# The first weight group behind three norms, multiplied one token tile at a time

## The chip, the cores and the metric

The kernel runs on one core of one Trainium2 chip. The metric is the device time of one execution in microseconds, as the median of several runs. A profile of one execution stands beside it.

## The reference

Two transformer-like blocks run one after the other on 256 tokens of width 1024, all in float32. What matters here is the place where a residual stream is normed and then multiplied by weights. In short:

```
# block 1
hx = modulate(rmsnorm(x, pre_mix_g), sh1, sc1);  yx = mlstm_mixer(hx, hc, ...)
x  = x + g1 * rmsnorm(yx, post_mix_g)            # "post1"
hx = modulate(rmsnorm(x, pre_ffn_g), sh2, sc2)   # "norm2"
yx = (silu(conv3(hx @ up_gate)) * (hx @ up_u)) @ down_w
x  = x + g2 * rmsnorm(yx, post_ffn_g)            # "post2"
# block 2
h  = rmsnorm(x, attn_norm_w)                     # "norm3"
x  = x + (delta-rule heads and forgetting attention of h @ w_in) @ w_out
h  = rmsnorm(x, ffn_norm_w)                      # "norm4"
x  = x + (silu(h @ gate) * (h @ up)) @ w_down
x  = x + sigmoid(rmsnorm(x, ple_norm_w) @ w_ple_gate) * (p @ w_ple_proj)   # "norm5"
out = rmsnorm(x, final_norm_w)
```

## The kernel before

The 256 tokens are two token tiles of 128 (`TT = 2`); the width is eight slices `k` of 128 (`KD = 8`). Every product with a weight is made of three float32r products: the weight and the activation are each split in a high part (`w_hi`, `h_hi`) and a low remainder (`w_lo`, `h_lo`), and high times high, high times low and low times high are summed in PSUM. Weights come in groups of 1 MB through a ring of three buffers. For each group SyncE issues the DMA, ScalarE casts it to `w_hi` (L623 or L631), VectorE subtracts to get `w_lo` (L1141 or L1149), and TensorE multiplies. Each engine has one program written out by hand, and semaphores order them; an engine never goes past a wait.

A norm in front of a product goes like this. ScalarE takes sums of squares (L641), GpSimd makes the reciprocal root (L447 and L450), and VectorE scales the identity by it into `diag` (L1171), once per token tile. TensorE multiplies `x` by `diag`, which transposes and scales at once (`transposed`, L1845). ScalarE writes `h_hi` from PSUM with gain and shift (`hi_T`, L672 or L674), and VectorE writes `h_lo` (`transposed`, L1161 and L1162 for norm2, L1164 for norms 3 and 4). In all of this a step covers one slice `k` with both token tiles, 256 columns, and a PSUM bank holds two slices of both tiles. So `h_hi` can't begin before the transposes of token tile 1.

The first group behind a norm is multiplied in `feature_tiles` with `ready` set: 32 products with `h_hi` (L1819 and L1820), then 16 with `h_lo` (L1826), each with a 128x128 piece of weights standing in the array and 256 token columns moving. Norms 2 and 4 are followed by a loop over pairs of groups (`ffn`, `rounds`: three rounds of three pairs as a hardware loop, then two pairs written out), norm 3 by the groups of the `gdn` stage.

In front of norms 2 and 3 stands another norm (`post_norm`): VectorE multiplies the product in PSUM by a gain (L1178), and adds it, scaled, to `x` (L1188). It does so for tile 0 and then tile 1, since the last two weight groups in front of it are multiplied tile by tile. Norm 4 has only a residual sum in front of it (L1677).

Of the kernel before, what the change touches and what calls it, by code (L numbers as in the profile page):

```python
# [131 lines left out]
def two_blocks(nc, I, out):  # L132
# [5 lines left out]
    with ExitStack() as ctx:  # L138
# [20 lines left out]
        for kind, n in (("tr", KD // 2), ("hi", KD), ("hT", KD)):  # L159
            FAMILY[kind] = (("norm1", KD), ("y1", n), ("norm2", n), ("norm3", n), ("mix", KD // 2), ("norm4", n),  # L160
                            ("norm5", n))
# [192 lines left out]

        def in_round(s, r):


            return (s + 2 * ROUND * r, 0) if isinstance(r, int) else (s, r)

        def rounds(eng, step):  # L360

            with eng.Fori(0, ROUNDS) as r:
# [250 lines left out]
        def _(act):  # L613
# [35 lines left out]
            def post_norm(post, norm, product, bank0, updates):  # L649
# [26 lines left out]


# [149 lines left out]
            post_norm("post1", "norm2", "mix_out", 2, 0)  # L827
            hi_T("norm2", NORM_BANKS["norm2"], scale=lambda k: mod2[:, KD + k:KD + k + 1], shift=lambda k: mod2[:, k:k + 1])
# [22 lines left out]
            post_norm("post2", "norm3", "down", 4, 4)  # L851
# [9 lines left out]
            hi_T("norm3", NORM_BANKS["norm3"], lambda k: pcol("attn_norm", k))  # L861
# [187 lines left out]
            for i in range(4):  # L1049
                norm_half("norm4", 8, i, i // 2, i % 2)  # L1050
# [3 lines left out]
            hi_T("norm4", NORM_BANKS["norm4"], lambda k: pcol("ffn_norm", k))  # L1054
# [56 lines left out]
        def _(dve):  # L1111
# [61 lines left out]
            def post_norm(post, norm, gain, bank0):  # L1173
# [252 lines left out]
            post_norm("post1", "norm2", gp1, 2)  # L1426
            dve.sem_inc(S("act_full"), ROUND)
            transposed("norm2", NORM_BANKS["norm2"], lambda k: mod2[:, KD + k:KD + k + 1], lambda k: mod2[:, k:k + 1])
# [35 lines left out]
            post_norm("post2", "norm3", gp2, 4)  # L1464


            transposed("norm3", NORM_BANKS["norm3"], lambda k: pcol("attn_norm", k))
# [213 lines left out]
            transposed("norm4", NORM_BANKS["norm4"], lambda k: pcol("ffn_norm", k))  # L1681
# [46 lines left out]
        def _(pe):  # L1728
# [77 lines left out]
            def feature_tiles(s, bank, r=0, ready=None, between=None):  # L1806
# [5 lines left out]
                if ready is not None:  # L1812
                    for f in range(2):
                        fs_ = slice(f * P, (f + 1) * P)
                        for k in range(KD):
                            if f == 0:
                                pe.wait_ge(S("hi"), base("hi", ready) + k + 1)
                            dst = ps[:, bank, f * T:(f + 1) * T]
                            pe.matmul(dst, hi[:, k, fs_], h_hi[:, k, :], start=f == k == 0, stop=False)  # L1819
                            pe.matmul(dst, lo[:, k, fs_], h_hi[:, k, :], start=False, stop=False)  # L1820
                    for f in range(2):
                        fs_ = slice(f * P, (f + 1) * P)
                        for k in range(KD):
                            if f == 0:
                                pe.wait_ge(S("hT"), base("hT", ready) + k + 1)
                            ins = pe.matmul(ps[:, bank, f * T:(f + 1) * T], hi[:, k, fs_], h_lo[:, k, :], start=False,  # L1826
                                            stop=f == 1 and k == KD - 1)
                    ins.then_inc(group_used, 1)
                    return
                for f in range(2):  # L1830
# [296 lines left out]
            def ffn(name, norm):  # L2127

                def step(r, u):
                    pe.wait_ge(S("act_full"), base("act_full", name) + ROUND * r + u + 1)  # L2130
                    for half in range(2):
                        feature_tiles(at[name][2 * u + half], 2 * u + half, r, norm if u == half == 0 else None)

                rounds(pe, step)
# [16 lines left out]
            transposed("norm2")  # L2151
# [4 lines left out]
            transposed("norm3")  # L2156
            def gdn_tiles(j, between=None):
# [3 lines left out]
                feature_tiles(at["gdn"][j], j % 2, ready="norm3" if j == 0 else None, between=between)  # L2161
# [44 lines left out]
            gdn_tiles(0)  # L2206
# [192 lines left out]
            def att_out(i, t):  # L2399
# [5 lines left out]
                for kk in range(GH):  # L2405
                    if n == 0 and t == 0 and kk % 2 == 0:
# [41 lines left out]
            for t in range(TT):  # L2448
                att_out(2, t)
                att_out(3, t)  # L2450
# [49 lines left out]
```

## Time and profile before

| | us |
|---|---|
| median of 3 runs | 849.33 (847.73 to 855.03) |
| the profiled execution's own time | 849.84 |
| span of its profile, first to last instruction | 848.1 |
| TensorE matmul busy | 803.2 (95%) |
| VectorE busy | 509.9 (60%) |
| ScalarE busy | 386.2 (46%) |
| mean granted TensorE clock | 0.988 |

TensorE is busy nearly all the time, so what counts is where it stands idle, how long each matmul takes from one start to the next, and how many there are. Busy time of TensorE counts overlapping matmuls once, and their ends are modelled, so the start times in the timeline say more than the busy share.

### The profile page before, as it was taken

Reading aid. Unit: us, or ns where it says so; the run is one execution under the profiler, and the core shown is the slowest. Engines: PE = TensorE matmul, PEld = TensorE weight load, DVE = VectorE, ACT = ScalarE, POOL = GpSimd, SP = SyncE. Lnnn points to the kernel's source line nnn. Section 1 sums busy time; section 2 is a strip of 40 time slices with the busy share of each in tenths; the row PEclk is TensorE's granted clock in tenths of the full one; section 3 lists DMA queues with packets and bytes.
Section 4 is the critical chain, followed back from the end, with each engine's and each line's share of the span. In section 5 each row is a group of like instructions: output and inputs, shape, how many; then the busy total and the mean of one; then the engine's idle time right before and its main releaser. Section 6 shows DMA issues by size and latency. Waiting matters only on the chain. (4 is left out here: it accounts for less than half of the span.)

```text
span 848.1 us, 12688 instructions
## 1 busy us (share of the span) xinstructions
PE 803.2 (95%) x5135; PEld 711.2 (84%) x5135; DVE 509.9 (60%) x681; ACT 386.2 (46%) x522; POOL 105.6 (12%) x170
## 2 busy tenths in 40 slices
PE   3899999999899999999979999999999999999996
PEld 1678877777789999987779988988899999988885
DVE  0447789866676766686467884454464554554355
ACT  1533413344554565434366544546364344343373
POOL 3210221501100000000070314110100000000000
PEclk9999999999999999999999999999999999999999
DMA  9767377723165555577624343311455555455531
GB/s 329 271 205 278 123 256 258 278 71 96 54 199 188 166 169 186 185 274 271 189 80 133 100 149 100 100 51 50 149 187 176 172 197 189 162 170 196 175 100 49
DMA packets 102430, 142.74 MB, mean 168 GB/s; under 512 B 6248, under 2 KB 62065, under 8 KB 102385
## 3 DMA queue, kind: packets, MB, share of 16 engines
q1 hardware_dynamic: 96128, 136.33, 48.0%
q10 hardware_dynamic: 6192, 5.79, 2.2%
q8 instruction: 31, 0.51, 0.3%
q14 instruction: 15, 0.11, 0.0%
q0 software_dynamic: 64, 0.01, 0.0%
HBM read 141.05 MB, written 1.05 MB: 168 GB/s over the span
## 5 line engine op out<-in xcount | busy, mean ns | idle before, releaser
L1732 PE MATMUL ps<-h_hi,w_hi 128*128 128x256 f32 x720 | 205.2, 285 | 0.9 <-DVE w_lo L1141 0.9
L1733 PE MATMUL ps<-h_lo,w_hi 128*128 128x256 f32 x720 | 204.4, 284 | 0.0
L1734 PE MATMUL ps<-h_hi,w_lo 128*128 128x256 f32 x720 | 204.4, 284 | 0.0
L1141 DVE TENSOR_TENSOR w_lo<-raw,w_hi 128x2048 fp32r<-128x2048 f32 (+1 forms) x63 | 139.8, 2226 | 75.0 <-ACT w_hi L623 74.7
L623 ACT CAST w_hi<-raw 128x2048 fp32r<-128x2048 f32 (+1 forms) x63 | 116.8, 1854 | 101.4 <-PE ps L1734 56.5
L1732 PEld LDWEIGHTS ps<-h_hi,w_hi 128*128 128x128 f32 x720 | 138.9, 193 | 1.1 <-DVE w_lo L1141 1.1
L1733 PEld LDWEIGHTS ps<-h_lo,w_hi 128*128 128x128 f32 x720 | 138.9, 193 | 0.0
L1734 PEld LDWEIGHTS ps<-h_hi,w_lo 128*128 128x128 f32 x720 | 138.8, 193 | 0.0
L1149 DVE TENSOR_TENSOR w_lo<-raw,w_hi 128x2048 fp32r<-128x2048 f32 x44 | 100.7, 2290 | 61.4 <-ACT w_hi L631 61.4
L631 ACT CAST w_hi<-raw 128x2048 fp32r<-128x2048 f32 x44 | 83.6, 1899 | 52.6 <-PE ps L1734 52.6
L1732 PE MATMUL ps<-w_hi,h_hi 128*128 128x512 f32 x208 | 84.9, 408 | 2.8 <-DVE r L1342 1.6
L1733 PE MATMUL ps<-w_lo,h_hi 128*128 128x512 f32 x208 | 82.3, 396 | 0.0
L1734 PE MATMUL ps<-w_hi,h_lo 128*128 128x512 f32 x208 | 82.1, 395 | 0.0
L1732 PE MATMUL ps<-w_hi,act_hi 128*128 128x512 f32 x176 | 70.1, 398 | 0.0
L1733 PE MATMUL ps<-w_lo,act_hi 128*128 128x512 f32 x176 | 69.6, 395 | 0.0
L1734 PE MATMUL ps<-w_hi,act_lo 128*128 128x512 f32 x176 | 69.6, 395 | 0.0
L1732 PEld LDWEIGHTS ps<-w_hi,h_hi 128*128 128x128 f32 x208 | 39.7, 191 | 15.6 <-issue 3.4
L1734 PEld LDWEIGHTS ps<-w_hi,h_lo 128*128 128x128 f32 x208 | 39.7, 191 | 8.8
L1733 PEld LDWEIGHTS ps<-w_lo,h_hi 128*128 128x128 f32 x208 | 39.7, 191 | 7.6
L447 POOL TENSOR_SCALAR ss<-ss 128x1 f32<-128x1 f32 x14 | 4.4, 315 | 301.1 <-ACT junk L641 300.9
L1732 PEld LDWEIGHTS ps<-w_hi,act_hi 128*128 128x128 f32 x176 | 33.1, 188 | 8.2 <-issue 0.2
L1733 PEld LDWEIGHTS ps<-w_lo,act_hi 128*128 128x128 f32 x176 | 33.1, 188 | 8.0 <-issue 0.2
(365 smaller groups left out, 1265.2 us busy)
## 6 DMA issues: line engine op xcount, KB each, us to landing
raw<-in_ada_w SPq DMA_DIRECT2D x24, 1024.0 KB, 5.5
raw<-in_ffn_up_w SPq DMA_DIRECT2D x22, 1024.0 KB, 5.1
raw<-in_w_gate_up SPq DMA_DIRECT2D x22, 1024.0 KB, 5.1
raw<-in_w_in SPq DMA_DIRECT2D x14, 1024.0 KB, 5.2
raw<-in_m_in_w SPq DMA_DIRECT2D x12, 1024.0 KB, 5.2
raw<-in_ffn_down_w SPq DMA_DIRECT2D x10, 1024.0 KB, 5.2
raw<-in_w_down SPq DMA_DIRECT2D x10, 1024.0 KB, 5.0
raw<-in_m_out_w SPq DMA_DIRECT2D x4, 1024.0 KB, 5.4
```

Of the source, the lines that this page charges most:

```text
L447: link(pool.tensor_scalar(s, s, ss[:, c0 + TT:c0 + TT + 1], EPS, ALU.add, ALU.add))
L623: act.copy(part_view(w_hi, s), raw_view(split[s])).then_inc(hi_ready, 1)
L631: act.copy(part_view(w_hi, s), raw_view(split[s])).then_inc(hi_ready, 1)
L1141: dve.tensor_tensor(part_view(w_lo, s), raw_view(split[s]), part_view(w_hi, s).bitcast(F32), ALU.subtract).then_inc(lo_ready, 1)
L1149: dve.tensor_tensor(part_view(w_lo, s), raw_view(split[s]), part_view(w_hi, s).bitcast(F32), ALU.subtract).then_inc(lo_ready, 1)
L1732: pe.matmul(dst, l_hi, r_hi, start=first, stop=False)
L1733: pe.matmul(dst, l_hi, r_lo, start=False, stop=False)
L1734: return pe.matmul(dst, l_lo, r_hi, start=False, stop=last)
```

## The change

Behind norms 2, 3 and 4 the work goes by token tile. The transposes of tile 0 go to two PSUM banks and those of tile 1 to two others (`tile_bank`). `h_hi` and `h_lo` are written for 128 columns at a time (`tile_hi`, `tile_lo`), with twice as many instructions, and the first weight group is multiplied first with tile 0 and then with tile 1: 2 x 48 matmuls of 128 columns where there were 48 of 256 (`first_group`). ScalarE writes tile 0's `h_hi` between the sums of squares of tile 1's product and of tile 1's `x`. VectorE writes six of the eight `h_lo` slices of tile 0 after tile 1's `x` update, then makes tile 1's `diag`, then the last two. In norm 4 the transposes of tile 0 stand in the middle of the last part of the attention's output product (`att_out(3, 1, between)`), and VectorE makes `diag` and `h_lo` of tile 0 ahead of tile 1's residual sum. In TensorE's program the first round of the two `ffn` loops is written out, since only it has the first group; the rounds that follow use the plain order of products.

```
+        def tile_bank(name, t, k):
+            return ps[:, NORM_BANKS[name][2 * t + k // 4], k % 4 * P:(k % 4 + 1) * P]
...
-        def rounds(eng, step):
+        def rounds(eng, step, unrolled=0):
+            for r in range(unrolled):
+                for u in range(ROUND):
+                    step(r, u)
+            with eng.Fori(unrolled, ROUNDS) as r:
...
# ScalarE, post_norm
                         sum_sq(ps[:, bank0 + 2 * n + t, :], SS[post] + TT * n + t)
+                        if n == t == 1:
+                            tile0_hi()
                         if n == 1:
                             for half in range(2):
                                 norm_half(norm, updates, 2 * t + half, t, half)
...
+            def tile_hi(name, t, scale, shift=None):
+                tok = slice(t * P, (t + 1) * P)
+                for k in range(KD):
+                    act.wait_ge(S("tr"), base("tr", name) + 2 * t + k // 4 + 1)
+                    src = tile_bank(name, t, k)
+                    if shift is None:
+                        ins = act.activation(h_hi[:, k, tok], src, ACT.Copy, scale=scale(k))
+                    else:
+                        ins = act.activation(h_hi[:, k, tok], src, ACT.Identity, scale=scale(k), bias=shift(k))
+                    ins.then_inc(S("hi"), 1)
...
# ScalarE, norm 4
-            for i in range(4):
-                norm_half("norm4", 8, i, i // 2, i % 2)
+            for i in range(2):
+                norm_half("norm4", 8, i, 0, i)
+            tile_hi("norm4", 0, lambda k: pcol("ffn_norm", k))
+            for i in range(2, 4):
+                norm_half("norm4", 8, i, 1, i - 2)
...
# VectorE
+            def tile_lo(name, t, scale, shift=None, ks=range(KD)):
+                tok = slice(t * P, (t + 1) * P)
+                for k in ks:
+                    dve.wait_ge(S("hi"), base("hi", name) + t * KD + k // 4 * 4 + 4)
+                    src = tile_bank(name, t, k)
+                    hi = h_hi[:, k, tok].bitcast(F32)
+                    if shift:
+                        link(dve.tensor_scalar(full[:, k, tok], src, scale(k), shift(k), ALU.mult, ALU.add))
+                        ins = dve.tensor_tensor(h_lo[:, k, tok], full[:, k, tok], hi, ALU.subtract)
+                    else:
+                        ins = dve.scalar_tensor_tensor(h_lo[:, k, tok], src, scale(k), hi, ALU.mult, ALU.subtract)
+                    ins.then_inc(S("hT"), 1)
...
# VectorE, post_norm, behind the x updates of tile t
+                    if t == 1:
+                        tile0_lo(range(0, 6))
                     diagonal(norm, t, base("rstd", post) + 2 * t + 2)
+                tile0_lo(range(6, KD))
...
# VectorE, norm 4, in the loop of residual sums over t
-            for t in range(TT):
-                diagonal("norm4", t, base("rstd", "norm4") + t + 1)
+                if t == 0:
+                    diagonal("norm4", 0, base("rstd", "norm4") + 1)
+                    tile_lo("norm4", 0, lambda k: pcol("ffn_norm", k))
+            diagonal("norm4", 1, base("rstd", "norm4") + 2)
...
# TensorE
+            def tile_turned(name, t):
+                pe.wait_ge(S("diag"), base("diag", name) + t + 1)
+                for k in range(KD):
+                    ins = pe.matmul(tile_bank(name, t, k), x[:, t, k * P:(k + 1) * P], diag[:, t, :], start=True, stop=True)
+                    if k % 4 == 3:
+                        ins.then_inc(S("tr"), 1)
+
+            def tile_products(name, t, s, bank):
+                hi, lo = weights(s)
+                tok = slice(t * P, (t + 1) * P)
+                for k in range(KD):
+                    pe.wait_ge(S("hi"), base("hi", name) + t * KD + k + 1)
+                    for f in range(2):
+                        dst, fs_ = ps[:, bank, f * T + t * P:f * T + (t + 1) * P], slice(f * P, (f + 1) * P)
+                        pe.matmul(dst, hi[:, k, fs_], h_hi[:, k, tok], start=t == f == k == 0, stop=False)
+                        pe.matmul(dst, lo[:, k, fs_], h_hi[:, k, tok], start=False, stop=False)
+                for k in range(KD):
+                    pe.wait_ge(S("hT"), base("hT", name) + t * KD + k + 1)
+                    for f in range(2):
+                        dst, fs_ = ps[:, bank, f * T + t * P:f * T + (t + 1) * P], slice(f * P, (f + 1) * P)
+                        ins = pe.matmul(dst, hi[:, k, fs_], h_lo[:, k, tok], start=False, stop=t == f == 1 and k == KD - 1)
+                return ins
+
+            def first_group(name, s, bank, turned=0):
+                for t in range(TT):
+                    if t >= turned:
+                        tile_turned(name, t)
+                    ins = tile_products(name, t, s, bank)
+                ins.then_inc(group_used, 1)
...
# TensorE, att_out(3, 1): the last product ahead of norm 4
-                att_out(3, t)
-            transposed("norm4")
-            ffn("gate_up", "norm4")
+                att_out(3, t, (lambda: tile_turned("norm4", 0)) if t else None)
+            ffn("gate_up", "norm4", 1)
```

## Rows read from the trace of the kernel before

**Rows 1.** The page, part 1: busy time, share of the span, instructions.

```profile
PE 803.2 (95%) x5135; PEld 711.2 (84%) x5135; DVE 509.9 (60%) x681; ACT 386.2 (46%) x522; POOL 105.6 (12%) x170
```

**Rows 2.** Waits: who waited for whom, us in total, times, longest.

```profile
PE ps L1845 <- DVE diag L1171: 10.0, 5, 3.3
PEld ps L1732 <- issue: 3.7, 6, 1.5
```

**Rows 3.** Timeline of TensorE at norm 2: start, us, line, out<-in, count, idle before.

```profile
220.32 2.05 PE L1845 MATMUL ps<-diag,x 128*128 128x128 f32 x16 [0.35 <-DVE diag L1171]
225.64 2.76 PE L1845 MATMUL ps<-diag,x 128*128 128x128 f32 x16 [3.27 <-DVE diag L1171]
228.05 0.56 PE L1819 MATMUL ps<-h_hi,w_hi 128*128 128x256 f32 x1
...
237.12 0.58 PE L1732 MATMUL ps<-h_hi,w_hi 128*128 128x256 f32 x1 [0.87 <-DVE w_lo L1141]
```

**Rows 4.** Timeline of ScalarE and VectorE at norm 2.

```profile
222.75 0.63 ACT L641 ACTIVATE junk<-x 128x512 f32<-128x512 f32 x1 [1.99 <-DVE x L1188]
226.39 3.76 ACT L674 ACTIVATE h_hi<-ps,mod 128x256 fp32r<-128x256 f32 x8 [0.23 <-PE ps L1845]
...
221.90 1.41 DVE L1188 SCALAR_TENSOR_TENSOR x<-full,rstd,x 128x512 f32<-128x512 f32 x2 [0.42 <-POOL rstd L450]
227.44 0.54 DVE L1161 TENSOR_SCALAR full<-ps,mod 128x256 f32<-128x256 f32 x1 [1.86 <-ACT h_hi L674]
...
234.78 4.49 DVE L1141 TENSOR_TENSOR w_lo<-raw,w_hi 128x2048 fp32r<-128x2048 f32 x2
```

**Rows 5.** Windows: us, busy by engine, granted clock, DMA share, GB/s.

```profile
228.00:230.20 2.20, 2.20 (x12) 2.20 (x12) 2.11 (x6) 2.20 (x6) 0.00 (x0) 0.50 0.00 0
```

**Rows 6.** Groups of instructions by shape: busy us, mean ns of one, idle before.

```profile
L1733 PE MATMUL ps<-h_lo,w_hi 128*128 128x256 f32 x720 | 204.4, 284 | 0.0
L1733 PE MATMUL ps<-w_lo,h_hi 128*128 128x512 f32 x208 | 82.3, 396 | 0.0
L1732 PEld LDWEIGHTS ps<-h_hi,w_hi 128*128 128x128 f32 x720 | 138.9, 193 | 1.1 <-DVE w_lo L1141 1.1
L1929 PEld LDWEIGHTS ps<-h_lo,wg_parts 128*32 128x32 f32 x16 | 1.7, 108 | 0.1
L641 ACT ACTIVATE junk<-ps 128x512 f32<-128x512 f32 x8 | 4.8, 598 | 10.0 <-PE ps L1734 9.9
L641 ACT ACTIVATE junk<-ps 128x128 f32<-128x128 f32 x8 | 2.2, 276 | 2.1 <-PE ps L2441 1.9
L1585 DVE SCALAR_TENSOR_TENSOR r<-ps,neg_c 128x256 f32<-128x256 f32 x8 | 3.3, 415 | 0.0
L1585 DVE SCALAR_TENSOR_TENSOR r<-ps,neg_c 128x128 f32<-128x128 f32 x8 | 2.3, 291 | 17.8 <-PE ps L2290 17.8
```

**Rows 7.** Timeline of TensorE's weight loads early in the kernel.

```profile
32.63 0.97 PEld L1885 LDWEIGHTS ps<-row_of,r 128*128 128x128 f32 x8 [0.19 <-DVE r L1204]
```

**Rows 8.** Timeline of TensorE at norms 3 and 4.

```profile
425.89 2.05 PE L1845 MATMUL ps<-diag,x 128*128 128x128 f32 x16 [1.75 <-DVE diag L1171]
431.04 3.31 PE L1845 MATMUL ps<-diag,x 128*128 128x128 f32 x16 [3.10 <-DVE diag L1171]
...
440.27 0.28 PE L1929 MATMUL ps<-h_hi,wg_parts 128*32 128x256 f32 x1
...
616.03 4.21 PE L1845 MATMUL ps<-diag,x 128*128 128x128 f32 x32 [1.57 <-DVE diag L1171]
...
626.20 0.28 PE L1732 MATMUL ps<-h_hi,w_hi 128*128 128x256 f32 x1
```

**Rows 9.** Timeline of ScalarE and VectorE at norms 3 and 4.

```profile
427.59 0.63 ACT L641 ACTIVATE junk<-x 128x512 f32<-128x512 f32 x1 [2.40 <-DVE x L1188]
432.17 3.05 ACT L672 ACTIVATE h_hi<-ps,cols 128x256 fp32r<-128x256 f32 x8 [1.17 <-PE ps L1845]
...
614.49 1.29 DVE L1677 TENSOR_TENSOR x<-x,ps 128x512 f32<-128x512 f32 x2 [4.15 <-PE ps L1734]
```

More of the change, by code:

```diff
@@ L647, in norm_half, with post_norm @@
                 sum_sq(x[:, t, n * NB:(n + 1) * NB], SS[name] + TT * n + t)
-            def post_norm(post, norm, product, bank0, updates):
+            def post_norm(post, norm, product, bank0, updates, tile0_hi):
                 for n in range(2):
@@ L826, in _, with norm2_hi @@
             hi_T("y1", (0, 1, 0, 1), lambda k: pcol("m_norm", k), pairs=range(MH - 1, MH))
-            post_norm("post1", "norm2", "mix_out", 2, 0)
-            hi_T("norm2", NORM_BANKS["norm2"], scale=lambda k: mod2[:, KD + k:KD + k + 1], shift=lambda k: mod2[:, k:k + 1])
+            def norm2_hi(t):
+                tile_hi("norm2", t, lambda k: mod2[:, KD + k:KD + k + 1], lambda k: mod2[:, k:k + 1])
+            post_norm("post1", "norm2", "mix_out", 2, 0, lambda: norm2_hi(0))
+            norm2_hi(1)
             U0 = at["up"][0]
@@ L1425, in _, with norm2_lo @@
             lo_until(at["mix_out"][1] + 3)
-            post_norm("post1", "norm2", gp1, 2)
+            def norm2_lo(t, ks=range(KD)):
+                tile_lo("norm2", t, lambda k: mod2[:, KD + k:KD + k + 1], lambda k: mod2[:, k:k + 1], ks)
+            post_norm("post1", "norm2", gp1, 2, lambda ks: norm2_lo(0, ks))
             dve.sem_inc(S("act_full"), ROUND)
-            transposed("norm2", NORM_BANKS["norm2"], lambda k: mod2[:, KD + k:KD + k + 1], lambda k: mod2[:, k:k + 1])
+            norm2_lo(1)
             def up_half(u):
@@ L1463, in _, with norm3_lo @@
             lo_until(at["down"][1] + 6 + 1)
-            post_norm("post2", "norm3", gp2, 4)
-            transposed("norm3", NORM_BANKS["norm3"], lambda k: pcol("attn_norm", k))
+            def norm3_lo(t, ks=range(KD)):
+                tile_lo("norm3", t, lambda k: pcol("attn_norm", k), ks=ks)
+            post_norm("post2", "norm3", gp2, 4, lambda ks: norm3_lo(0, ks))
+            norm3_lo(1)
             G0 = at["gdn"][0]
@@ L1804, in token_block, with feature_tiles @@
                                 ins.then_inc(S("t0_done"), 1)
-            def feature_tiles(s, bank, r=0, ready=None, between=None):
+            def feature_tiles(s, bank, r=0, between=None):
                 s, r = in_round(s, r)
@@ L1811, in feature_tiles @@
                 hi, lo = part_view(w_hi, s), part_view(w_lo, s)
[L1812 to L1829, printed above, removed]
                 for f in range(2):
@@ L2125, in _, with ffn @@
             token_block(at["mix_out"][1], [(*X0, 4), (*X1, 5)], tail="t0_done")
-            def ffn(name, norm):
+            def ffn(name, norm, turned=0):
                 def step(r, u):
+                    first = isinstance(r, int) and r == u == 0
+                    if first:
+                        first_group(norm, at[name][0], 0, turned)
                     pe.wait_ge(S("act_full"), base("act_full", name) + ROUND * r + u + 1)
-                    for half in range(2):
-                        feature_tiles(at[name][2 * u + half], 2 * u + half, r, norm if u == half == 0 else None)
-                rounds(pe, step)
+                    for half in range(first, 2):
+                        feature_tiles(at[name][2 * u + half], 2 * u + half, r)
+                rounds(pe, step, 1)
             def second(name, first, hi, lo, before_last=None):
@@ L2160, in gdn_tiles @@
                     pe.wait_ge(S("conv2_done"), 2 * (j - 1))
-                feature_tiles(at["gdn"][j], j % 2, ready="norm3" if j == 0 else None, between=between)
+                feature_tiles(at["gdn"][j], j % 2, between=between)
             def to_tokens(i, t, bank):
@@ L2204, in fox_tiles @@
                 feature_tiles(at["fox"][m], m if m < 2 else 3)
-            gdn_tiles(0)
+            first_group("norm3", at["gdn"][0], 0)
             gates_by_row(2, ((h_hi, h_lo),))
@@ L2397, in mix_pair, with att_out @@
                 ins.then_inc(S("tr"), 1)
-            def att_out(i, t):
+            def att_out(i, t, between=None):
                 half, n = i // 2, i % 2
@@ L2405, in att_out @@
                 for kk in range(GH):
+                    if between is not None and kk == GH // 2:
+                        between()
                     if n == 0 and t == 0 and kk % 2 == 0:
```

19 lines of the change are left out of this document (9 added, 10 removed).

## The prediction, made before the changed kernel ran

> **What bounds the kernel now.** The page's table of engines comes first: TensorE is busy 803.2 of 848.1 us [rows 1], so the time is TensorE's stream of matmuls plus its idle places. The list of waits says where these are: TensorE waits 10.0 us in all for `diag` [rows 2], the longest entry that this change can touch. The timeline shows each. At norm 2 it stops for 0.35 us before tile 0's transposes and 3.27 us before tile 1's, and later 0.87 us for `w_lo` [rows 3]. At norm 3 it stops for 1.75 and 3.10 us, at norm 4 for 1.57 us [rows 8]. The change wants to fill these holes with products of tile 0. So the question is what each stage of norm and first group takes before and after, read between two fixed marks: the end of the product before the norm, and the start of what follows the first group. These stages are 219.97 to 237.12 for norm 2 (17.15 us), 424.14 to 440.27 for norm 3 (16.13 us) and 614.46 to 626.20 for norm 4 (11.74 us); each first mark is the start of the first transposes less their idle time [rows 3, 8].
>
> **What a 128-column product costs.** This carries the sum. Before, the group is 48 matmuls of 256 columns; after, 96 of 128. If halves cost half, nothing is lost. No float32r matmul of 128 columns stands in the trace. The transposes give the rate of one float32 piece: the code has 8 matmuls per tile, the row counts 16 records, and 16 in 2.05 us with the last one some 0.27 long are 0.118 us from start to start [rows 3]. The weights decide more. A float32r load of 128 columns lasts 193 ns, one of 32 columns 108 ns [rows 6]: 85 ns for 96 columns, 0.89 ns a column, so 128 columns occupy the loading path for some 0.11 us. The weight loads of L1885, whose matmuls move almost nothing, confirm it: 8 in 0.97 us, less 0.19 for the last, over 7 is 0.111 us each [rows 7]. A matmul that brings its own 128 columns of weights therefore can't follow the last in less than 0.111 us, whether it moves 256 columns or 128. At 256 the moving columns and the load just cover each other; at 128 the load is alone on the path. From below the price is bounded by the moving columns: 396 against 284 ns for 512 and 256 columns [rows 6] is 0.056 us per 128 columns, so 0.118 less 0.056 makes 0.062 us. From above by the transposes' own form, which does 128 columns in two records: 0.236 us. I take 0.111 us, since the load durations are of the very same weights. The group then takes 96 x 0.111 = 10.7 us where it took 48 x 0.118 = 5.7 us: 5.0 us more TensorE work per norm, against holes of 4.5, 4.9 and 1.6 us.
>
> The Trainium skill speaks against this price. "TensorE: Matmul & The Clock Gate", section "Back-to-back issue gap", gives some 81 ns for each load and matmul at 128 columns in a real kernel. An estimate by that page is 96 x 0.081 = 7.8 us for the group, which by the steps below would make norm 4 0.1 us shorter, norm 3 1.2 us shorter and leave norm 2, for 850 us. No row here has that operation; the rows of float32 and float32r loads stand against it.
>
> **Narrow steps on the other engines.** ScalarE's 8 `h_hi` slices of norms 3 and 4 start every 0.367 us, those of norm 2 every 0.455 us (3.76 less 0.58, over 7) [rows 4, 9]. 128 columns fewer save 0.107 us (598 against 276 ns for 384 columns [rows 6]): 0.26 and 0.35 us. VectorE's pair for norm 2 takes 0.918 us (227.44 to 234.78 for eight [rows 4]); 128 columns fewer save 0.124 us in each of two (415 against 291 ns [rows 6]): 0.66 us. The single step of norms 3 and 4 is 0.27 us, from the 291 ns of its narrow relative and a short overlap. All counts double.
>
> **Norm 4.** Tile 0's transposes move in front of the last six matmuls of the attention's output product. Their `diag` can be ready: tile 0's residual sums ended at 610.34 (614.49 less 4.15 idle [rows 9]), and sums of squares and root need about 2 us. So 1.9 us of transposes fill no hole here; they push the product's end to 616.4. VectorE then does tile 1's residual sum behind tile 0's `h_lo`, which waits for ScalarE, to 618.5 (before: 615.8); `diag` of tile 1 follows at 620.7. TensorE has tile 0's 48 products meanwhile, 616.3 to 621.6, so it never waits. Its stage is pure work: 32 records x 0.118 = 3.8 and 10.7, 14.4 us against 11.74. **+2.7 us**.
>
> **Norm 3.** The hole of 1.75 us stays. ScalarE now does tile 0's `h_hi`, which waits for the transposes until 427.0, and ends at 429.1; only then the sums of squares of tile 1's `x`, which started at 427.59 [rows 9]: 1.5 us late, and `diag` of tile 1 with them (432.5). Behind it VectorE has slices 6 and 7 of tile 0, and TensorE's program puts tile 1's transposes behind these: it waits some 0.3 us and starts them at 433.4, where they started at 431.04. The stage is 1.75 + 14.4 + 0.3 = 16.5 us. **+0.4 us**. That counts the full clock throughout: the slow transposes of tile 1 (3.31 us for what takes 2.05 [rows 8]) came after 3.1 us of idling, which is gone.
>
> **Norm 2.** Here VectorE ends last. Its `x` update ends at 223.31 [rows 4]. Then six slices x 0.66 = 3.9 us, to 227.3; tile 1's root has been ready since about 226.9, as its squares start 1.5 us later than at 222.75 [rows 4]; `diag` 227.5; two slices, 228.9. TensorE follows with two products and starts tile 1's transposes at 229.1, where they started at 225.64. Their first four slices are out at 230.2, four `h_hi` at 231.7; VectorE, idle for 2.8 us, does 8 x 0.66 = 5.3 us, to 237.0, and `w_lo` of the second group (2.24 us, half of 4.49 [rows 4]) at 239.2. The second group started at 237.12. **+2.0 us**. The bounds are the clock: before, the stretch 228.0 to 230.2 had 0.50 granted, which is 1.2 GHz [rows 5], after the idling of 3.27 us, and the second group began slow too (0.58 us for its first matmul [rows 3]). After the change TensorE is thinly busy twice, when it follows VectorE's slices. Slow there: up to 1.5 us more; fast at the start of the second group: 1.6 us less.
>
> **The loops.** Writing out the first round changes no instruction that runs but the order in the first groups of the next rounds, 256 columns wide as before: nothing. The waits list has TensorE held up by no fetch at loop turns; its longest "issue" entry for weights is 1.5 us [rows 2], so 0 to 1.5 us bounds this too, and I take 0. Sixteen more waits per norm cost nothing that a row shows.
>
> **Sum.** 2.7 + 0.4 + 2.0 = 5.1 us. On the profiled execution's own 849.84 us that is 854.9; the median of before lies 0.5 lower, so 849.33 + 5.1 = 854.4 us, 0.6% slower. A measurement of this kernel can tell about 1% from no change, so this counts as no change.
>
> **The rivals.** (a) **Halves cost half** (0.062 us). Group 6.0 us. Norm 4 is then bound by ScalarE and VectorE behind `diag` at 620.7, ending at 625.3 (-0.9); norm 3 by the `h_lo` of tile 1, at 437.9 (-2.4); norm 2 still by VectorE (+2.0). 848.0 us. For it: moving columns do scale [rows 6]. Against it: the weight loads. (b) **A narrow float32r product runs like the float32 transposes**, 0.236 us. Group 22.7 us, stage 26.4: +14.7, +12.0 (with the hole), and norm 2 at 26.8 - 17.15 = +9.6. 885.6 us. This is the slower side; from 0.142 us on (14 us more in the three groups) it counts as slower. For it: the trace has no narrow float32r matmul at all, and the only narrow form has this rate. Against it: nothing in the load and move rows asks for it. (c) **The clock stays low** where TensorE follows VectorE slice by slice, in norms 2 and 3 and into the next group: one such stretch doubled tile 1's loads of norm 3 for a loss of 1.3 us (3.31 against 2.05 us [rows 8]); with three or four of these on top of the forecast, 859 us. (d) **The overlap does all that it can**: the holes of 4.5, 4.9 and 1.6 us filled and the slow stretches gone, with products at 0.062 us: at most 13 us, 838 us. Against it: tile 1's `diag` gets later in all three norms, by 1.5 to 2.6 us.
>
> **Chances.** Forecast 0.62, (a) 0.14 (with the page's 850 us in it), (b) 0.10, (c) 0.09, (d) 0.05. Leaving out (b) and (d) leaves 0.85; the range reaches from (a), 848.0 less 1.5 for the clock, to (c) and its own spread: 846.5 to 861. Faster by over 1% (below 840.8) is (d): 0.05. Slower by over 1% (above 857.8) is (b), most of (c), and the forecast's tail at 0.118 us a matmul with a slow stretch: 0.23. Within 1%: 0.72.
>
> **What would show it.** The matmuls of the first groups start 0.11 us apart. The sums of squares of tile 1's `x` come some 1.5 us later behind tile 0's transposes. In norm 2 the second group waits for `w_lo`; in norm 4 TensorE has no hole at all and the stage is 14.4 us. I am wrong if the spacing is 0.06 or 0.24, or if the granted clock is 0.50 in the tile 0 products.

## The result, and the profile after

The changed kernel takes 857.41 us (median of 8 runs, 856.14 to 860.12), the kernel before 850.9 us (median of 8) on the same chip. The ratio of the runs is 1.0088 with an interval of 1.0067 to 1.011, which is 7.5 us more; the two medians lie 6.5 us apart. The forecast was 854.4 us, no change by the bound of 1%. The ratio stays below that bound, but its interval reaches over it. Every experiment's ratio below is against the kernel before on the same chip as itself, and a single execution of b3 that ran much slower than all others (1009.23 us at a mean granted clock of 0.751) counts in its median but not in its ratio. The profiled execution took 858.67 us at a span of 856.9. Part 1 of its page, against [rows 1]:

```profile
PE 817.7 (95%) x5279; PEld 726.8 (85%) x5279; DVE 514.4 (60%) x713; ACT 390.4 (46%) x546; POOL 103.9 (12%) x170
```

TensorE has 144 instructions more (3 norms x 48) and 14.5 us more busy time: it works through the holes, and the kernel is not faster for it. The waits, against [rows 2]:

```profile
PE ps L2150 <- DMA acc<-in_ada_b: 2.3, 1, 2.3
PE ps L1881 <- DVE diag L1202: 2.1, 2, 1.8
PE ps L1788 <- DVE w_lo L1172: 1.9, 1, 1.9
```

The 10.0 us of waiting for `diag` have shrunk to 2.1: the change does what it says. A wait of 1.9 us for `w_lo` has come up, the one that the prediction named for norm 2. TensorE's timeline at norm 2, against [rows 3] (start, us, instruction, idle before it):

```profile
219.47 2.05 PE L1881 MATMUL ps<-diag,x 128*128 128x128 f32 x16 [0.35 <-DVE diag L1202]
...
227.91 0.44 PE L1899 MATMUL ps<-h_lo,w_hi 128*128 128x128 f32 x2 [0.21 <-DVE h_lo L1213]
228.18 3.34 PE L1881 MATMUL ps<-diag,x 128*128 128x128 f32 x16
...
232.27 0.27 PE L1893 MATMUL ps<-h_hi,w_hi 128*128 128x128 f32 x1
232.38 0.27 PE L1894 MATMUL ps<-h_hi,w_lo 128*128 128x128 f32 x1
...
239.01 0.55 PE L1788 MATMUL ps<-h_hi,w_hi 128*128 128x256 f32 x1 [1.85 <-DVE w_lo L1172]
```

The narrow products start 0.11 us apart, as forecast (232.27 to 232.38). Tile 1's transposes start at 228.18, 8.7 us behind tile 0's; before it was 5.3 us (225.64 less 220.32 [rows 3]). They are slow (3.34 us for the usual 2.05), and the windows say why. Their columns: the stretch, its length, busy time and instructions of TensorE, its weight loads, VectorE, ScalarE and GpSimd, then granted clock, busy share of the DMA engines and GB/s.

```profile
223.00:228.50 5.50, 4.69 (x38) 4.26 (x38) 4.61 (x16) 3.88 (x7) 0.94 (x2) 1.00 0.00 0
228.60:231.90 3.30, 3.30 (x19) 3.30 (x17) 0.47 (x2) 1.85 (x5) 0.00 (x0) 0.50 0.00 0
232.00:237.00 5.00, 5.00 (x46) 5.00 (x45) 4.76 (x16) 2.85 (x5) 0.00 (x0) 1.00 0.00 0
238.90:242.10 3.20, 3.09 (x14) 3.12 (x15) 3.05 (x4) 3.18 (x4) 0.00 (x0) 0.50 0.59 192
395.90:399.10 3.20, 3.20 (x7) 1.89 (x6) 1.68 (x3) 1.30 (x1) 0.00 (x0) 0.50 0.77 238
...
424.92:448.62 23.70, 21.95 (x175) 20.65 (x174) 15.58 (x31) 14.53 (x35) 14.41 (x24) 1.00 0.24 59
616.00:635.00 19.00, 19.00 (x151) 18.17 (x149) 9.54 (x24) 10.95 (x26) 1.75 (x4) 1.00 0.33 111
```

Tile 1's transposes ran at a granted clock of 0.50, 1.2 GHz, although TensorE had been busy for 4.69 of the 5.50 us ahead of them. The next group's start ran at 0.50 too, as it did before (0.58 us for its first matmul [rows 3]), and so did a stretch near 396 us, between norms 2 and 3. In norms 3 and 4 the clock is full, and in norm 4 TensorE is busy for 19.00 of 19.00 us: no hole at all. ScalarE and VectorE at norm 2, against [rows 4]:

```profile
220.73 2.91 ACT L695 ACTIVATE h_hi<-ps,mod 128x128 fp32r<-128x128 f32 x8 [0.82 <-PE ps L1881]
223.49 0.67 ACT L647 ACTIVATE junk<-x 128x512 f32<-128x512 f32 x1
...
226.28 0.28 DVE L1202 TENSOR_SCALAR diag<-ident,rstd 128x128 f32<-128x128 f32 x1
...
231.39 0.41 DVE L1212 TENSOR_SCALAR full<-ps,mod 128x128 f32<-128x128 f32 x1 [3.54 <-ACT h_hi L695]
...
236.58 4.49 DVE L1172 TENSOR_TENSOR w_lo<-raw,w_hi 128x2048 fp32r<-128x2048 f32 x2
```

ScalarE squares tile 1's `x` only when tile 0's eight `h_hi` are out. The pair of VectorE steps takes 0.65 us for 128 columns (231.39 to 236.58 for eight; forecast 0.66). VectorE then stands idle for 3.54 us, where 2.8 were forecast. Part of this is the clock: in b3 and b12 below the same transposes took 2.00 us, and VectorE's idle time was 3.02 and 3.01 us. TensorE at norms 3 and 4, against [rows 8], then ScalarE and VectorE behind norm 3:

```profile
430.83 2.05 PE L1881 MATMUL ps<-diag,x 128*128 128x128 f32 x16 [1.75 <-DVE diag L1202]
...
438.12 2.00 PE L1881 MATMUL ps<-diag,x 128*128 128x128 f32 x16
...
445.27 0.28 PE L2000 MATMUL ps<-h_hi,wg_parts 128*32 128x256 f32 x1
...
627.81 2.00 PE L1881 MATMUL ps<-diag,x 128*128 128x128 f32 x16
...
634.96 0.34 PE L1788 MATMUL ps<-h_hi,w_hi 128*128 128x256 f32 x1
```

```profile
439.27 2.18 ACT L693 ACTIVATE h_hi<-ps,cols 128x128 fp32r<-128x128 f32 x8 [1.70 <-PE ps L1881]
```

```profile
440.44 2.16 DVE L1215 SCALAR_TENSOR_TENSOR h_lo<-ps,cols,h_hi 128x128 fp32r<-128x128 f32 x8 [2.90 <-ACT h_hi L693]
443.46 0.29 DVE L1184 TENSOR_TENSOR wg_parts<-wsm,wg_parts 128x128 fp32r<-128x128 f32 x1 [0.86 <-ACT wg_parts L893]
443.67 5.02 DVE L1172 TENSOR_TENSOR w_lo<-raw,w_hi 128x2048 fp32r<-128x2048 f32 x2
448.62 2.93 DVE L1531 SCALAR_TENSOR_TENSOR r<-ps,cols,r 128x255 f32<-128x255 f32 x6
```

**Where the time went.** The same instruction is looked up in each trace, which gives a table of stages (us between starts; read from the timelines). The marks are VectorE's first product with the gain in norm 2 (A) and in norm 3 (C), its first `cv` behind norm 2 (B), its first `r<-ps,cols,r` behind norm 3 (D; 448.62 above), its first residual sum ahead of norm 4 (E), its first `act_lo` behind it (F), and the end.

```
kernel                     A-B     B-C     C-D     D-E     E-F    F-end
before                    24.80  180.79   22.23  166.85   27.24  211.77
after                     27.45  183.93   23.70  166.85   29.66  211.77
b1  all three back        24.80  180.28   22.21  166.84   27.24  211.78
b2  norm 2 back           25.23  179.61   23.69  166.83   29.66  211.78
b3  norm 3 back           26.93  181.24   22.13  168.46   29.66  211.78
b4  norm 4 back           27.68  182.95   23.70  166.87   27.24  211.78
b12 norm 2 only           26.91  181.69   22.01  166.81   27.23  211.77
b5  wide products         26.33  179.32   24.81  166.84   32.46  211.78
b10 wide, filled          25.41  179.15   22.78  167.02   30.04  211.78
b7  casts ahead           25.71  178.59   23.06  168.80   27.24  211.77
b8  casts and repeats     25.69  177.83   21.21  168.28   27.24  211.76
b9  repeats               24.81  178.88   22.24  166.84   27.23  211.78
b11 b1 and repeats        24.79  181.48   22.21  166.79   27.24  211.78
```

The pair before and after differs by 2.65 us in norm 2 (A-B), 3.14 behind it (B-C), 1.47 in norm 3 and 2.42 in norm 4, less 0.84 by which after reached A earlier: 8.8 us. These are single profiles, and the granted clock falls to 0.50 at different places in them. It did so between D and E in b3 (at 510 us), b7 (at 511 us) and b8 (at 502 us) alone, which are the three with 168.3 to 168.8 us there instead of 166.8 to 167.0. Mark A itself lies anywhere from 213.5 to 218.4 us, though everything that the kernels have changed comes behind it. What of the 8.8 us is the change's own, the experiments tell.

### The profile page after: what moved, and what is told of

The parts are those of the page before. It is cut to its first block and busy times, and to the rows that moved or that the text cites. A ratio compares the mean times of both kernels' runs of the same rounds, so it can differ in the third digit from the quotient of the medians.

```text
span 856.9 us, 13015 instructions
## 1 busy us (share of the span) xinstructions
PE 817.7 (95%) x5279; PEld 726.8 (85%) x5279; DVE 514.4 (60%) x713; ACT 390.4 (46%) x546; POOL 103.9 (12%) x170
## 5 line engine op out<-in xcount | busy, mean ns | idle before, releaser
L1788 PE MATMUL ps<-h_hi,w_hi 128*128 128x256 f32 x816 | 232.5, 285 | 1.9 <-DVE w_lo L1172 1.9
L1789 PE MATMUL ps<-h_lo,w_hi 128*128 128x256 f32 x816 | 231.6, 284 | 0.0
L1790 PE MATMUL ps<-h_hi,w_lo 128*128 128x256 f32 x816 | 231.5, 284 | 0.0
L1788 PEld LDWEIGHTS ps<-h_hi,w_hi 128*128 128x128 f32 x816 | 156.1, 191 | 2.0 <-issue 2.0
L1789 PEld LDWEIGHTS ps<-h_lo,w_hi 128*128 128x128 f32 x816 | 156.1, 191 | 0.0
L1790 PEld LDWEIGHTS ps<-h_hi,w_lo 128*128 128x128 f32 x816 | 156.1, 191 | 0.0
```

The source lines that it names most:

```text
L1788: pe.matmul(dst, l_hi, r_hi, start=first, stop=False)
L1789: pe.matmul(dst, l_hi, r_lo, start=False, stop=False)
L1790: return pe.matmul(dst, l_lo, r_hi, start=False, stop=last)
```

## The experiments

**One norm taken back at a time** (b2 to b4; b1 takes all three back, b12 has the change in norm 2 only). Each kernel is the changed one with a test in the code; for norm 2 back:

```diff
+OLD = ("norm2",)
             def first_group(name, s, bank, turned=0):
+                if name in OLD:
+                    transposed(name)          # both tiles
+                    wide_products(name, s, bank, 0)   # 48 x 256 columns
+                    return
```

and ScalarE's and VectorE's `tile0_hi`, `tile0_lo` left out for that norm.

> The changed kernel with norms 2, 3 and 4 multiplied as before; what stays of the change is only the unrolled first round of the loops. Theory (the cost is in the three norms alone): level with the kernel before, ratio 0.999 to 1.001, and TensorE waits about 0.8 us for the third slice of the bias before the gate vectors, as in the profile of before. Rival (the code layout or the unrolled round costs): the wait of 2.3 us and the 1.6 us of the down stage stay, ratio 1.002 to 1.003.

Measured: 849.64 us against 850.45, ratio 0.9985 (0.9965 to 1.0005). All six stages stand within 0.6 us of before, and the wait for the bias (`acc<-in_ada_b`) is 0.2 us instead of the 2.3 of after. The ratio lies a hair below the theory's band and its interval reaches into it; the rival's 1.002 lies outside. The unrolled round costs nothing.

> The changed kernel with norm 2 as before, norms 3 and 4 by token tile. Of the 7.5 us that the change costs by the medians, additive theory: norm 2 carries 2.7 us, so 4.8 us are left, ratio 1.0055 (1.004 to 1.007). Rival (clock and queue state behind norm 2 carry the cost on, the down stage's 1.6 us with it): 3.2 us are left, ratio 1.0035 to 1.004.

Measured: 853.2 us, ratio 1.0046 (1.0029 to 1.0064): 3.9 us are left, which is what C-D (1.46) and E-F (2.42) of this very kernel add up to. Norm 2 so accounts for 7.5 less 3.9, 3.6 us, with some 2.4 us of uncertainty from the two intervals. The ratio lies in the theory's band, but the interval covers the rival's 1.0035 to 1.004 as well, so the total doesn't decide between the two.

> The changed kernel with norm 3 as before, norms 2 and 4 by token tile. Theory (VectorE comes out of norm 3 some 1.4 us later against TensorE than before, and the stage of the gated delta rule passes that on): 6 us are left, ratio 1.007, and the stretch from the end of norm 3's first group to norm 4's first square is 169.5 us instead of 170.9. Rival (norm 3 costs what its own stage shows, 0.1 us, and the 1.4 us have another cause): 7.4 us are left, ratio 1.009, and the stretch stays at 170.9.

Measured: 857.94 us, ratio 1.0099 (1.0073 to 1.0125), 8.4 us. The total settles nothing. The median of the five executions without the one of 1009.23 us is 856.42 us, 6.0 us above 850.45, just the theory's figure; the ratio is on the rival's side; and its interval, some 2.2 us to either side, is wider than the term of 1.5 us. The stages speak for the theory in part: C-D falls from 23.70 to 22.13 us, the 1.5 us. A stretch at a granted clock of 0.50 stands in D-E in this trace and costs 1.6 us there. The lost 1.5 us are in C-D and not, as the expectation put it, in the stretch behind: measured from VectorE's mark D, D-E is 166.85 us before and after. TensorE's mark at the end of the group, which I had used, lies ahead of them.

> The changed kernel with norm 4 as before, norms 2 and 3 by token tile. Theory (nothing stands still in norm 4, so that each float32r product of half the width at 0.111 us is a plain loss): norm 4 carries 2.4 us, 5.1 us are left, ratio 1.006 (1.005 to 1.007). Rival (the transposes inside the att_out group and ScalarE's changed order disturb more than that): 3.5 us or less are left, ratio 1.004 or below.

Measured: 857.29 us, ratio 1.0087 (1.0065 to 1.0108), no gain in the total. The stage E-F is 27.24 us, exactly before's, against 29.66 in every kernel with norm 4 by tile (after, b2, b3). So the 2.42 us are there. The profiled execution lost as much ahead of the first norm in question: it reached mark A at 216.61 us and after at 213.54, in the same code, with one more stretch at 0.50 ahead of A (at 143 us); between A and E it was 0.7 us shorter than after. Neither expectation of the ratio held. Two ratios with some 1.8 us of uncertainty each can't exclude a gain of 2.4 us; the stage is settled, the total isn't.

> The change in norm 2 alone; norms 3 and 4 as before. Additive theory (taking norm 2 back gave 3.6 us by the ratios 1.0088 and 1.0046): 2.7 to 3.6 us above the kernel before, ratio 1.003 to 1.0045. Rival (norm 2 in the new form also brings later stretches of low clock and waits, which taking back norms 3 and 4 did not remove): 5 us or more, ratio 1.006 or above.

Measured: 854.47 us, ratio 1.0054 (1.003 to 1.0078), 4.6 us, between theory and rival. A to C takes 208.2 to 211.4 us in the four kernels with norm 2 by tile (after, b3, b4, b12) and 204.8 to 205.6 in before, b1 and b2: 2.6 to 6.6 us more. Much of this spread is where the clock fell. In b3 and in b2 TensorE had a granted clock of 0.50 for 3.4 us between A and C, and they differ by 3.3 us (208.17 and 204.84); in b12 and in before for 6.9 us, and they differ by 3.0 (208.60 and 205.59). Against b1 and b11, with 6.8 us each, b12 is 3.5 and 2.3 us longer (205.08 and 206.27). In after and b4 it was 10 us, and after's share near 396 us stands in no other trace here. The wait for `acc<-in_ada_b`, 2.3 us in after, is 1.17 in b3, 1.63 in b4 and 0.94 in b12: after's 183.93 was partly chance. At like clock norm 2 so costs some 3 us, 2.3 to 3.5. Of this A-B holds 2.1 (b3 and b12, whose transposes of tile 1 took 2.00 us); it is 2.65 and 2.88 in after and b4, where they took 3.34 and 3.56 us. Why the stretch behind B is longer as well, by some 1 us, stays open.

**Wide products behind the tile-wise transposes** (b5).

```diff
-                    tile_turned(name, t)
-                ins = tile_products(name, t, s, bank)
+                for t in range(turned, TT):
+                    tile_turned(name, t)
+                wide_products(name, s, bank, KD)
```

> The changed kernel, its tile-wise transposes and high and low parts kept, but the 48 products of each first group taken over all 256 tokens behind tile 1, as before. Theory (the width of the products is what costs: 96 at 0.111 us against 48 at 0.118 us): norm 4 costs about 0.1 us instead of the 2.4 us of the changed kernel; norms 2 and 3 keep only what VectorE's and ScalarE's narrower instructions cost, 1 us and 1.5 us at most; ratio 1.000 to 1.003. Rival (the transposes by tile, placed inside the att_out group and behind the wait for each diagonal, cost it, not the width): norm 4 still costs 2 us or more, ratio 1.006 to 1.009.

Measured: 857.15 us, ratio 1.0079 (1.0053 to 1.0104), 6.7 us. The theory that the width alone costs falls: norm 4's stage is even longer, 32.46 us. TensorE's timeline of b5 at the three norms shows why (its rows of tile 1's transposes):

```profile
227.64 3.42 PE L1906 MATMUL ps<-diag,x 128*128 128x128 f32 x16 [5.09 <-DVE diag L1215]
...
432.90 3.78 PE L1906 MATMUL ps<-diag,x 128*128 128x128 f32 x16 [4.71 <-DVE diag L1215]
...
623.78 3.78 PE L1906 MATMUL ps<-diag,x 128*128 128x128 f32 x16 [4.71 <-DVE diag L1215]
```

Before, these waits were 3.27 and 3.10 us [rows 3, 8] and 1.57 us ahead of both tiles [rows 8]. The rival's ratio and its 2 us or more in norm 4 hold. The change makes its own holes larger, since ScalarE's `h_hi` of tile 0 and VectorE's `h_lo` stand ahead of tile 1's norm; then it fills them with products that together take nearly twice as long. Windows of b5, one for each norm, and the same of before below them (the granted clock stands behind POOL's count):

```profile
215.00:242.00 27.00, 20.21 (x129) 18.13 (x128) 20.81 (x47) 17.20 (x34) 3.59 (x8) 0.94 0.20 65
420.00:444.00 24.00, 17.53 (x106) 16.10 (x105) 14.86 (x30) 13.08 (x33) 14.35 (x26) 0.86 0.20 49
608.00:640.00 32.00, 27.29 (x170) 25.33 (x169) 17.02 (x27) 13.81 (x29) 1.75 (x4) 0.89 0.47 156
```

```profile
215.00:242.00 27.00, 21.77 (x130) 19.77 (x130) 19.53 (x33) 16.78 (x28) 3.48 (x8) 0.87 0.27 85
420.00:444.00 24.00, 19.15 (x130) 17.69 (x129) 16.50 (x26) 13.68 (x27) 16.12 (x27) 0.93 0.32 88
608.00:640.00 32.00, 30.32 (x225) 28.48 (x224) 16.58 (x21) 16.44 (x24) 1.74 (x4) 1.00 0.63 206
```

Behind its pauses of 4.71 us b5 also runs slow in norms 3 and 4. b10 fills them:

```diff
+                        if t == 1:
+                            for i in range(24 if name == "norm4" else 12):
+                                pe.matmul(ps[:, bank, ...], x[:, 0, ...], diag[:, 0, :], start=True, stop=True)
                         tile_turned(name, t)
```

> b5 (the changed kernel's transposes by tile with the products over 256 tokens), with 12 more transposes of tile 0, into the bank of the group's result, while TensorE waits for tile 1's diagonal in norms 2 and 3, and 24 in norm 4, where b5 stands for 4.7 us. Theory (b5 lost in the granted clock, 33 us of low clock in a run against 21, what its wide products saved): the mean clock rises from 0.981 to 0.988 or more, and the time comes to 1 to 3 us above the kernel before, ratio 1.001 to 1.004. Rival (b5's time has its cause in the transposes by tile themselves, with the clock only a companion): ratio 1.006 to 1.009 as b5.

Measured: 853.49 us, ratio 1.0042 (1.0025 to 1.0059), just above the theory's upper end, which the interval covers. All three windows of b10 stand at full clock:

```profile
215.00:242.00 27.00, 22.89 (x161) 20.57 (x160) 21.58 (x48) 18.13 (x35) 3.58 (x8) 1.00 0.23 75
420.00:444.00 24.00, 20.21 (x157) 18.89 (x156) 16.27 (x33) 14.93 (x34) 15.44 (x25) 1.00 0.32 89
608.00:640.00 32.00, 32.00 (x250) 30.90 (x249) 17.65 (x29) 15.75 (x30) 1.75 (x4) 1.00 0.54 182
```

Useless work in the pauses gave back 3.7 us by the medians and 3.1 by the ratios. Followed by wide products and filled with repeats, norm 4 takes 30.04 us, with tile 0's real products in the pause 29.66. Of these 0.4 us the repeats themselves cost 0.5: tile 1's transposes start 12.40 us behind mark E in b10 (621.41) and 11.91 in b5 (623.78), with E at 609.01 and 611.87. At full clock the two ways are level. In after they start 12.35 us behind E, so even without any product of tile 0 they could start only 0.44 us earlier; what holds them is tile 1's `diag`, which VectorE makes 11.57 us behind E where it was 8.79 before. These are VectorE's rows of that `diag`, before and after:

```profile
617.85 0.29 DVE L1171 TENSOR_SCALAR diag<-ident,rstd 128x128 f32<-128x128 f32 x1 [1.87 <-POOL rstd L450]
...
627.03 0.29 DVE L1202 TENSOR_SCALAR diag<-ident,rstd 128x128 f32<-128x128 f32 x1 [2.01 <-POOL rstd L456]
```

The real products in the pause buy nothing, since tile 1's 48 take 5.4 us behind it (to 19.50 us behind E) where all 48 wide ones of b10 take 5.8. Both halves of the price are needed for this: the late `diag`, and products of half the width that cost as much as whole ones.

**Which size sets the pace of a product** (b6). It leaves out half of each tile's tokens in norm 2's group and half of the features in norm 3's.

```diff
-                tok = slice(t * P, (t + 1) * P)
+                cols_, feats = (64, P) if name == "norm2" else (P, 64) if name == "norm3" else (P, P)
+                tok = slice(t * P, t * P + cols_)
-                        dst, fs_ = ps[:, bank, ...], slice(f * P, (f + 1) * P)
+                        dst, fs_ = ps[0:feats, bank, ...], slice(f * P, f * P + feats)
```

> The changed kernel with smaller products in two first groups, which leaves out half of the tokens of each tile in norm 2's group and half of the features in norm 3's. Norm 2: 128 weight columns with 64 token columns. Norm 3: 64 weight columns with 128 token columns. Theory (the load of the weights sets the pace, one column after another): norm 2's products stay 0.107 to 0.111 us apart, norm 3's fall to 0.055 to 0.065 us. Rival 1 (a fixed cost of each instruction sets it): both stay at 0.107 to 0.111 us. Rival 2 (the columns that move set it): norm 2's fall to about 0.06 us and norm 3's stay at 0.111 us.

Measured: its timeline of TensorE, norm 2 (128 weight columns, 64 moving), then norm 3 (64 weight columns, 128 moving):

```profile
234.86 0.28 PE L1895 MATMUL ps<-h_hi,w_lo 128*128 128x64 f32 x1
234.97 0.28 PE L1894 MATMUL ps<-h_hi,w_hi 128*128 128x64 f32 x1
...
439.07 0.22 PE L1894 MATMUL ps<-h_hi,w_hi 128*64 128x128 f32 x1
439.13 0.22 PE L1895 MATMUL ps<-h_hi,w_lo 128*64 128x128 f32 x1
```

With half the moving columns the starts stay 0.11 us apart; with half the weight columns they are 0.06 apart. The load of 128 weight columns sets the pace; both rivals fall. At 64 weight columns the pace can't be put down to one of the two: 0.06 us is half of the load, and the estimate for 128 moving columns from [rows 6] is 0.056 as well.

**Better use of the pauses in the kernel before** (b7, b8, b9, b11). b7 casts the next group's weights ahead of tile 1's norm; b9 repeats tile 0's transposes; b8 does both; b11 is b1 with b9's repeats.

```diff
 # b7
                         sum_sq(ps[:, bank0 + 2 * n + t, :], SS[post] + TT * n + t)
+                        if n == t == 1:
+                            hi_until(done + 2)
...
+                    if t == 1:
+                        lo_until(ahead)
                     diagonal(...)
 # b9
-                    for k in range(KD):
+                    for k in (*range(KD), *(range(4) ...), *(range(KD) ...)):   # t == 0, norms 2 and 3
```

> The kernel before, with the casts of the next group's weights moved ahead: ScalarE's high part of the first two pieces behind the sum of squares, VectorE's low part behind the update of tile 1 and before its diagonal. Theory (VectorE's low part of the weights is what norm 2's second group waits for, and what VectorE is behind by after norm 3): norm 2 gains 0.9 to 2 us, norm 3 nothing in its stage and up to 1 us behind it; ratio 0.997 to 0.999. Rival (there is no room ahead of the diagonal, which comes later by what the casts take): the hole in norm 2 grows by 1 us or more, ratio 1.001 to 1.004.

> As the last kernel, and TensorE repeats the transposes of tile 0 once and a half (12 more products of 128 columns) while it waits for tile 1's diagonal in norms 2 and 3. Theory (the stretches at half the granted clock in norms 2 and 3 follow TensorE's idle time there): the granted clock stays 1.0 through norm 3 and through norm 2's group, and 1 to 1.7 us come back for each stretch that goes, ratio 0.994 to 0.998. Rival (the stretches come whatever TensorE does in the hole): the same number of stretches as in the kernel before, and the ratio of the last kernel.

> The kernel before with 12 more transposes of tile 0 on TensorE while it waits for tile 1's diagonal, in norms 2 and 3, and nothing else. Theory (the stretches at half the granted clock in norms 2 and 3 come from TensorE's pauses there): norm 2's two and norm 3's one are gone in the profiled run, the mean clock rises from 0.988 to 0.991 or more, ratio 0.995 to 0.998. Rival (the two casts moved ahead did it in b8, not the repeated transposes): stretches as in the kernel before, ratio 0.999 to 1.001.

> b1 (norms as before, first round of the loops unrolled) with the repeated transposes of b9. Theory (the unrolled round is worth about 1 us, as b1's median says, and adds to the clock's part): ratio 0.994 to 0.997, 1 us below b9. Rival (b1's 0.9985 was chance): the same as b9 to 0.001.

Measured: b7 850.45 us, ratio 0.9995 (0.9979 to 1.0011); b8 847.83 us, 0.9975 (0.9958 to 0.9993); b9 850.43 us, 1.0005 (0.9989 to 1.0021); b11 850.52 us, 0.9999 (0.9987 to 1.001). Windows of b9 at norms 2 and 3, then VectorE behind norm 3:

```profile
215.00:242.00 27.00, 24.12 (x159) 20.96 (x158) 19.67 (x31) 15.26 (x26) 3.50 (x8) 1.00 0.19 60
420.00:444.00 24.00, 21.82 (x161) 19.97 (x161) 16.59 (x26) 14.53 (x28) 16.07 (x27) 1.00 0.32 86
```

```profile
437.60 4.75 DVE L1141 TENSOR_TENSOR w_lo<-raw,w_hi 128x2048 fp32r<-128x2048 f32 x2
442.27 2.93 DVE L1477 SCALAR_TENSOR_TENSOR r<-ps,cols,r 128x255 f32<-128x255 f32 x6
```

The slow stretches of both norms are gone here, where before had 0.87 and 0.93. For norm 3 this holds in every trace: the window is at 1.00 in b8, b9 and b11, which have the repeats, and a stretch at 0.50 stands in before, b1, b3, b7 and b12, which have the old norm 3 without them. That it follows TensorE's pause is well supported there. For norm 2 it isn't: b11, with the same repeats, ran slow at the start of the next group (its window of norm 2):

```profile
215.00:242.00 27.00, 24.05 (x149) 21.34 (x149) 19.57 (x32) 17.04 (x26) 3.16 (x7) 0.89 0.29 96
```

In norm 3 C-D stays at 22.24 us even so: the two casts on VectorE end last there, whatever TensorE's clock. Norm 2's part (A to C) is 203.69 us in b9 and 206.27 in b11, against 204.8 to 205.6, and the medians show no gain. b9's mean clock rose as its theory said, and its ratio is the rival's. b7 has neither its theory's ratio nor its rival's. It took a cast off the end, but the wait for tile 1's `diag` in norm 3 grew from 3.10 to 4.16 us, with a granted clock of 0.50 behind it, as these two rows of b7 show (timeline of TensorE, then a window), and the stage took 23.06:

```profile
434.79 3.78 PE L1849 MATMUL ps<-diag,x 128*128 128x128 f32 x16 [4.16 <-DVE diag L1173]
```

```profile
434.00:438.00 4.00, 3.21 (x15) 3.21 (x16) 1.81 (x4) 1.92 (x5) 3.58 (x7) 0.50 0.60 167
```

Only together do they shorten norm 3's stage, to 21.21. b8 is the fastest kernel here, 2.1 us under before by the ratio, in the band of its theory; that is a quarter of a per cent, and the interval just excludes 1. b11 doesn't repeat b1's small lead, so nothing speaks for that lead being real.

## Why the prediction came out as it did

**The cost of a 128-column product: right.** 0.111 us was taken, 0.11 us is what the rows show, and b6 shows the reason to be the load. Rival (a), 0.062 us for 128 moving columns, is reached only with 64 weight columns; rival (b), 0.236 us, is excluded. The 81 ns of the Trainium skill ("TensorE: Matmul & The Clock Gate", section "Back-to-back issue gap") do not hold for this float32r pair of load and matmul: 0.11 us in all three groups.

**Norm 4: right.** +2.7 forecast, +2.42 measured in three kernels to 0.01 us, without a hole as said. But "pure work" is half of the reason. The prediction put the end of tile 0's products 0.9 us behind tile 1's `diag` (621.6 and 620.7), and TensorE came 0.44 us later than the `diag` would have let it. The two paths end almost together, and shortening the work alone, as b5 and b10 did, gained nothing.

**The loops: right**, nothing (b1, b11).

**Norm 3: the sum stopped one engine too early.** The forecast of +0.4 was for TensorE's stage, which took 16.19 us (429.08 to 445.27) against 16.13. But the step counted only TensorE. Before, TensorE needed 5.05 us from ScalarE's last `h_hi` (435.22 [rows 9]) to the end of the group, 440.27; after, with tile 0 done, 3.82 us (441.45 to 445.27). The casts that ScalarE and VectorE owe the next groups stand behind the same `h_hi` and take as long as ever: from there to mark D 6.99 us before (to 442.21, its `r<-ps,cols,r`) and 7.17 after (to 448.62). TensorE's lead over them is what the overlap bought, and the next stage, which VectorE starts, doesn't use it. Mark D, not the end of TensorE's group, is the fixed mark: +1.47 to +1.69 us (23.70 and 23.69 against 22.23 to 22.01).

**Norm 2: right in its stage, too small as a whole.** VectorE ends last and the second group waits for `w_lo`, as said. A-B is 2.1 us longer than before's 24.80 at full clock (b3, b12), against +2.0. The prediction named the clock as a bound of up to 1.5 us and took none of it; where tile 1's transposes were slow (after, b4) it cost 0.5 to 0.8 us. The slow start of the next group, for whose going the bound allowed 1.6 us, did not go away but moved behind it in three of the four kernels. What the sum left out is the stretch behind mark B, some 1 us at like clock. By the ratios norm 2 costs 3.6 us (b2), alone 4.6 (b12), by the stages at like clock 2.3 to 3.5.

**The sum.** 5.1 us forecast. By the stages some 3 (2.3 to 3.5), 1.5 and 2.4 make 6.2 to 7.4, against 6.5 by the medians and 7.5 by the ratio. (That b2's 3.6 and 3.9 make 7.5 says nothing, since 3.6 is 7.5 less 3.9.) So the sum was short by about 2 us, some 1 in norm 3 and some 1 in norm 2. The median of before was 849.33 us in the three runs shown and 850.9 in eight; this accounts for 1.6 of the 3.0 us between 854.4 and 857.41. That the change counts as no change is partly luck: the interval of the ratio reaches 1.011.

**The rivals and slips.** Rival (c) falls as it was stated: where TensorE follows VectorE slice by slice (223.00:228.50) the clock was 1.00. It fell behind that, and added its part to the forecast. The argument against (d), that tile 1's `diag` gets later in all norms, proved to be the main effect. From the marks A, C and E the `diag` comes 1.8, 1.6 and 2.8 us later than before, and b5 shows it as waits of 5.09, 4.71 and 4.71 us. Two figures of the prediction don't follow from its own terms. Taking 13 us off 849.33 is 836.3 and not 838. And by its bound of 857.8 us a matmul would count as slower from about 0.13 us on, not 0.142: 3.4 us over the forecast, spread over the 192 products of norms 3 and 4. Neither bears on the forecast.

**Still open:** why b3's ratio and b4's median show no gain though their stages do; what lengthens the stretch behind norm 2; and what decides where the granted clock falls. The stretches at 0.50 fell differently in the profiled executions; that they did in the others too is likely, since their mean clocks differ, but no trace of them is kept.

## What to carry to other kernels

Splitting a matmul along its moving columns doesn't halve it when each piece brings its own weights: if the load alone already takes as long as the whole product did (0.111 us against 0.118), the first half in a pause leaves the second as long as the whole was. Before filling a pause, ask what the filler's inputs cost on the engines that end it; here they lengthened norm 3's from 3.10 to 4.71 us (b5). And set the marks of a stage where the next stage really starts, which may be another engine.

## What was not expected of the hardware

Products with 64 weight columns and 128 moving ones ran 0.06 us apart, those with 128 and 64 columns 0.11: with 128 weight columns, moving fewer than 128 columns gains nothing. The granted clock fell to 0.50 at 228.6 us although TensorE had been busy for 4.69 of the 5.50 us before; so standing still is not the only thing ahead of such a fall. In b3 and b12 the same instructions ran there at full clock (2.00 us for the transposes), so the same code meets either. And here a low clock cost nothing where another engine ended last: b9 removed norm 3's slow stretch, and the stage took 22.24 us against 22.23. In b3 such a stretch fell on a busy TensorE at 510 us, and D-E took 1.6 us longer.
